# Norms between the phases of the first block of a two-block transformer kernel: where their squares, scales and sums are placed

## What is computed

```python
def rms_norm(x, w):
    y = x * rsqrt(mean(x * x, -1) + 1e-6)
    return y * w

for i in range(2):
    a_in = rms_norm(hs, norm_w[i, 0])
    mix = gated_deltanet(a_in, ...) if i == 0 else mlstm(a_in, ...)
    hs = hs + keep * rms_norm(mix, norm_w[i, 1])
    f = conv_ffn(rms_norm(hs, norm_w[i, 2]), w_up, conv_w, conv_b, w_down)
    hs = hs + keep * rms_norm(f, norm_w[i, 3])

def conv_ffn(h, w_up, conv_w, conv_b, w_down):      # 3 taps along the tokens
    u = causal_depthwise_conv(h @ w_up, conv_w) + conv_b
    return (silu(u[..., :2816]) * u[..., 2816:]) @ w_down
```

## Time and profile before

| | us |
|---|---|
| median of 3 runs | 1733.51 (1730.83 to 1734.56) |
| the profiled execution | 1733.33 |
| its span, first to last instruction | 1731.4 |
| TensorE busy | 1550.3 (90%) |
| VectorE busy | 970.8 (56%) |
| ScalarE busy | 788.9 (46%) |
| GpSimd busy | 338.4 (20%) |
| mean granted TensorE clock | 0.931 of full |

### The profile page before, as it was taken

The page is one execution under the profiler, slowest core; times in us unless marked ns, Lnnn a source line. Parts: engine busy times, 40 slices in busy tenths (PEclk is TensorE's granted clock), DMA queues, the critical chain, the costliest instruction groups (busy, mean ns, idle before and its releaser), DMA issues.

```text
span 1731.4 us, 32148 instructions
## 1 busy us (share of the span) xinstructions
PE 1550.3 (90%) x11757; PEld 1465.3 (85%) x11757; DVE 970.8 (56%) x1486; ACT 788.9 (46%) x1308; POOL 338.4 (20%) x351
## 2 busy tenths in 40 slices
PE   6999979979999899877999978689999985889997
PEld 5997967869999879576999978589999773789997
DVE  5874846546775454345777454554544546454443
ACT  5565423445554455335555344354443542454433
POOL 1203001104552000002665010013320002023300
PEclk9998958999999999778999989799999995899999
DMA  5551300233556425022555535036666430346662
GB/s 202 177 171 60 110 26 1 88 108 124 179 179 179 141 97 173 23 73 58 176 178 175 179 110 170 26 119 184 182 186 187 137 114 1 98 122 182 182 188 67
DMA packets 60992, 222.04 MB, mean 128 GB/s; under 512 B 6768, under 2 KB 7792, under 8 KB 60528
## 3 DMA queue, kind: packets, MB, share of 16 engines
q1 hardware_dynamic: 60768, 219.75, 41.6%
q10 hardware_dynamic: 144, 1.18, 0.2%
HBM read 219.85 MB, written 1.05 MB: 128 GB/s over the span
## 4 chain that ended last, share of the span: by engine, by line
PE 84%; DVE 9%; ACT 3%; issue 2%; DMA 1%; POOL 0%; SPq 0%; ACTq 0%; DVEq 0%
PE bank L404 23%; PE bank L406 23%; PE bank L405 23%; PE bank L467 3%; DVE y L537 1%; DVE y L495 1%; PE bank L1661 1%; PE bank L1772 1%; DVE wlo L370 1%; PE bank L1875 1%; PE bank L1856 1%; DVE y L1815 1%; PE bank L1062 1%; DMA par<-params 1%; PE bank L1042 1%
## 5 line engine op out<-in xcount | busy, mean ns | idle before, releaser
L370 DVE TENSOR_TENSOR wlo<-raw,whi 128x1024 fp32r<-128x1024 f32 x411 | 514.1, 1261 | 466.1 <-ACT whi L365 465.8
L404 PE MATMUL bank<-xs,whi 128*128 128x272 f32 (+1 forms) x2264 | 654.4, 289 | 29.8 <-POOL xs L396 19.4
L405 PE MATMUL bank<-xs,whi 128*128 128x272 f32 (+1 forms) x2264 | 651.7, 288 | 0.0
L406 PE MATMUL bank<-xs,wlo 128*128 128x272 f32 (+1 forms) x2264 | 650.2, 287 | 0.0
L365 ACT ACTIVATE whi<-raw 128x1024 fp32r<-128x1024 f32 x411 | 429.1, 1055 | 286.2 <-PE bank L406 282.8
L404 PEld LDWEIGHTS bank<-xs,whi 128*128 128x128 f32 x2264 | 431.6, 191 | 34.5 <-issue 22.9
L406 PEld LDWEIGHTS bank<-xs,wlo 128*128 128x128 f32 x2264 | 433.4, 191 | 0.0
L405 PEld LDWEIGHTS bank<-xs,whi 128*128 128x128 f32 x2264 | 433.0, 191 | 0.0
L404 PE MATMUL bank<-hf,whi 128*128 (+2 forms) x1024 | 295.0, 288 | 11.5 <-issue 10.5
L405 PE MATMUL bank<-hf,whi 128*128 (+2 forms) x1024 | 294.4, 288 | 0.0
L406 PE MATMUL bank<-hf,wlo 128*128 (+2 forms) x1024 | 294.1, 287 | 0.0
(11 more groups left out here) (410 smaller groups left out, 1288.0 us busy)
## 6 DMA issues: line engine op xcount, KB each, us to landing
raw<-stream SPq DMA_DIRECT2D x411, 512.0 KB, 3.6
con<-consts SPq DMA_DIRECT2D x1, 1284.5 KB, 7.8
big<-mla ACTq DMA_DIRECT2D x1, 1152.0 KB, 4.9
hs_sb<-hs SPq DMA_DIRECT2D x1, 1088.0 KB, 5.1
y_out<-hs_sb SPq DMA_DIRECT2D x8, 128.0 KB, 2.0
par<-params SPq DMA_DIRECT2D x1, 740.0 KB, 9.1
```

The source lines that it names most:

```text
L370: nc.vector.tensor_tensor(wlo[:, s, :], raw[:, s, :], whi[:, s, :].bitcast(F32), ALU.subtract).then_inc(block_split, 1)
L404: nc.tensor.matmul(out_, whi[:, slot, w], hi, start=start, stop=False)
L405: nc.tensor.matmul(out_, whi[:, slot, w], lo, start=False, stop=False)
L406: return nc.tensor.matmul(out_, wlo[:, slot, w], hi, start=False, stop=stop)
```

## The change

Seven parts; all but the second concern the first block only.

1. **Squares in the last row.** In a wide phase's last row each bank m is marked when its three matmuls are done; ScalarE squares it straight from the bank, and TensorE puts the sum matmul of bank m - 3 behind bank m's matmuls; four sums are left behind the row. VectorE scales the bank by the norm's weight while moving it to `y`, after its square. The last low half of a wide phase moves behind these eight.
2. **Three tiles k by k.** In every tiles phase the first three tiles run side by side: for chunk k high x high and low x high of all three (six matmuls), as soon as the high half of the chunk is there, and one step later the three matmuls with its low half. The other tiles follow as before, from tile 3.
3. **The residual.** VectorE alone adds: product with the factor, then the sum, chunk by chunk; ScalarE takes from it the high half, scaled by the next norm's weight, and the square.
4. **The pre norm's factor comes later.** The tiles get hs x weight without the factor; its sums run inside the three tiles' steps, and the factor is put on the finished banks: in up0 and up1 VectorE multiplies each bank in place before the convolution's first tap, in ml_in VectorE evicts every tile with the product.
5. **ml_in's gates** take hs and weights that GpSimd scales beforehand, behind the three tiles; five of the first tiles' low halves and evictions are put between the steps of the scans; the sigmoid runs in place behind VectorE's eviction.
6. **GpSimd** has no part of these norms any more (it keeps pre0 and the layer norms).
7. One explicit table load per boundary goes.

The diff, cut to its core:

```diff
-    def pe_tiles(pe, phase, g0, name, count=None):
+    def pe_tiles(pe, phase, g0, name, count=None, meanwhile=lambda k: None):
...
+        for k in range(KC + 1):
+            if k < KC:
+                w = slice(k * P, (k + 1) * P)
+                pe.wait_ge(*S("norm", "act").at(f"{name}_hi{k}"))
+                for j in range(AHEAD):
+                    o, s = rhs_out(g0 + j, phase), (b0 + j) % SLOTS
+                    if k == 0:
+                        pe.wait_ge(block_split, b0 + j + 1)
+                        pe.wait_ge(bank_free, g0 + j + 1)
+                    mm(o, whi[:, s, w], xs[:, k, 0:T], start=(k == 0), stop=False)
+                    mm(o, wlo[:, s, w], xs[:, k, 0:T], start=False, stop=False)
+            if k:
+                meanwhile(k - 1)
+                w = slice((k - 1) * P, k * P)
+                pe.wait_ge(*lo_done(name, k - 1))
+                for j in range(AHEAD):
+                    last = mm(rhs_out(g0 + j, phase), whi[:, (b0 + j) % SLOTS, w], xs[:, KC + k - 1, 0:T], start=False, stop=(k == KC))
+                    if k == KC:
+                        last.then_inc(block_used, 1)
...
+                if i is None and k == n - 1 and m < 7:
+                    last.then_inc(*S("wide", "pe").mark(f"{phase}_m{m}"))
+                    meanwhile(m)
...
+    SUM_LAG = 3
...
+    def post_in_row(pe, name, g):
+        def meanwhile(m):
+            if m >= SUM_LAG:
+                square_sum_pe(pe, name, g, m - SUM_LAG)
...
+    def post_act(act, name, g, phase):
         for m in range(KC):
-            act.wait_ge(bank_free, 8 + g - 8 + m + 1)
-            nc.scalar.activation(sq[:, m, :], y[:, m, :], ACT.Square)...
+            wide_done(act, phase, m)
+            nc.scalar.activation(sq[:, m, :], bank[(g - 8 + m) % 8][:, 0:T1], ACT.Square)...
...
+    def post_dve(dve, name, g, row, split):
         for m in range(KC):
-            nc.vector.tensor_copy(y[:, m, :], bank[(g - 8 + m) % 8][:, 0:T1]).then_inc(bank_free, 1)
+            dve.wait_ge(*S("norm", "act").at(f"{name}_{m}"))
+            nc.vector.tensor_scalar(y[:, m, :], bank[(g - 8 + m) % 8][:, 0:T1], pv("norm_w", row * KC + m), None, ALU.mult).then_inc(bank_free, 1)
+        split()
...
+    def add_y(dve, name, m):
+        v = S("norm", "dve")
+        nc.vector.tensor_tensor(y[:, m, :], y[:, m, :], rs[:, 1, :], ALU.mult).then_inc(*v.mark(f"{name}_y{m}"))
+        dve.wait_ge(*v.at(f"{name}_y{m}"))
+        nc.vector.tensor_tensor(hs[:, m, :], hs[:, m, :], y[:, m, :], ALU.add).then_inc(*v.mark(f"{name}_h{m}"))
+
+    def next_dve(dve, post, name, row):
+        def lo(m):
+            dve.wait_ge(*S("norm", "act").at(f"{name}_hi{m}"))
+            nc.vector.scalar_tensor_tensor(xs[:, KC + m, :], hs[:, m, :], pv("norm_w", row * KC + m), xs[:, m, :].bitcast(F32),
+                                           ALU.mult, ALU.subtract)...
         for m in range(KC):
+            add_y(dve, post, m)
+            if m:
+                lo(m - 1)
+        lo(KC - 1)
+
+    def next_act(act, post, name, row, g):
+        for m in range(KC):
+            act.wait_ge(*S("norm", "dve").at(f"{post}_h{m}"))
+            nc.scalar.activation(xs[:, m, :], hs[:, m, :], ACT.Copy, scale=pv("norm_w", row * KC + m))...
+            nc.scalar.activation(sq[:, m, :], hs[:, m, :], ACT.Square)...
+        act_scale(act, name, g, rs[:, 0, :], T1, D, eps_1)
...
     def ffn_act(act, f, g0):
...
             split_hi(act, b0 + t + AHEAD, ii)
             split_hi(act, b0 + t + AHEAD + 1, ii)
-            act.wait_ge(block_used, ii * 8 + (b0 + t + 2))
             act.wait_ge(conv_taken, ii * 8 + (c0 + t + 2))
             if f < 2:
+                act.wait_ge(*S("ffn", "dve").at(f"u{f}_{base}_{j}1", i))
                 conv_first(st, f"f{f}_{base}_{j}", tiles, 3, True)
...
     def ffn_dve(dve, f, g0):
...
-            split_lo(dve, b0 + t + AHEAD, ii)
-            split_lo(dve, b0 + t + AHEAD + 1, ii)
+            for a in range(2):
+                split_lo(dve, b0 + t + a + AHEAD, ii)
+                if f < 2:
+                    dve.wait_ge(block_used, ii * 8 + (b0 + t + a + 1))
+                    u = tiles[a][0][:, 0:T1]
+                    nc.vector.tensor_tensor(u, u, rs[:, 0, :], ALU.mult).then_inc(*st.mark(f"u{f}_{base}_{j}{a}"))
...
+    def ml_tile_dve(dve, t, split=True, i=0):
+        if split:
+            split_lo(dve, b0 + t + AHEAD, i)
+        dve.wait_ge(block_used, i * 8 + (b0 + t + 1))
+        nc.vector.tensor_tensor(dst, bank[(g0 + t) % 8][:, 0:T1], rs[:, 0, :], ALU.mult).then_inc(bank_free, 1)
...
+        between = {1: 3, 4: 4, 7: 5}
+        b = scan(dve, s, "b", f_row, t4_row, ALU.add, T1, lambda n: ml_tile_dve(dve, between[n]) if n in between else None)
...
-        pre_pe(pe, "pre1", G["pre1"])
-        pe_tiles(pe, "up0", G["up0"], "pre1")
-        pe_wide(pe, "down0", G["down0"], ffn_ready(0))
+        pe_tiles_rest(pe, *pe_tiles(pe, "up0", G["up0"], "pre1", None, pre_in_wave("pre1")))
+        pe_wide(pe, "down0", G["down0"], ffn_ready(0), meanwhile=post_in_row(pe, "post1", G["post1"]))
```

More of the change, by code:

```diff
@@ L519, in mix_dve, with square_sum_pe @@
                                     ).then_inc(*S("norm", "dve").mark(f"{name}_lo{k}"))
+    SUM_LAG = 3
+    def square_sum_pe(pe, name, g, m):
+        if m == 0:
+            pe.wait_ge(bank_free, g + 1)
+        pe.wait_ge(*S("norm", "act").at(f"{name}_{m}"))
+        last = nc.tensor.matmul(bank[g % 8][:, 0:T1], ones, sq[:, m, :], start=(m == 0), stop=(m == KC - 1))
+        if m == KC - 1:
+            last.then_inc(*S("norm", "pe").mark(name))
+    def post_in_row(pe, name, g):
+        def meanwhile(m):
+            if m >= SUM_LAG:
+                square_sum_pe(pe, name, g, m - SUM_LAG)
+        return meanwhile
@@ L1571, in ml_gates_act, with scan @@
         A(s_row, s_row, ACT.Ln, bias=1.0).then_inc(*s.mark("lf"))
-    def scan(dve, s, tag, src, other, op, T):
+    def scan(dve, s, tag, src, other, op, T, meanwhile=lambda n: None):
         step, n = 1, 0
@@ L1588, in ml_gates_dve @@
         ts, stt, tt = nc.vector.tensor_scalar, nc.vector.scalar_tensor_tensor, nc.vector.tensor_tensor
+        for t in range(2):
+            split_lo(dve, FIRST_BLOCK["ml_in"] + t + AHEAD)
+        dve.wait_ge(*S("norm", "act").at("pre2_scale"))
+        for n, row in enumerate((i_row, f_row)):
+            dve.wait_ge(*S("gates", "pe").at(f"ml{n}"))
+            tt(row, bank[(G["ml_g"] + n) % 8][0:MH, 0:T1], rs[0:MH, 0, :], ALU.mult).then_inc(bank_free, 1)
+        ml_tile_dve(dve, 0, False)
+        ml_tile_dve(dve, 1, False)
+        ml_tile_dve(dve, 2)
         dve.wait_ge(*a_.at("lf"))
@@ L1594, in ml_gates_dve @@
         dve.wait_ge(*s.at("logf"))
-        b = scan(dve, s, "b", f_row, t4_row, ALU.add, T1)
-        split_all(dve, split_lo, "ml_in", 4, 4)
+        between = {1: 3, 4: 4, 7: 5}
+        b = scan(dve, s, "b", f_row, t4_row, ALU.add, T1, lambda n: ml_tile_dve(dve, between[n]) if n in between else None)
         stt(c_row, i_row, GATE_CAP, b, ALU.mult, ALU.subtract).then_inc(*s.mark("c"))
@@ L1606, in ml_in_act, with ml_gate_weights_pool @@
     def ml_in_act(act):
-        g0, b0 = G["ml_in"], FIRST_BLOCK["ml_in"]
-        for turn in range(2):
-            with act.Fori(0, (2, 1)[turn]) as i:
-                for j in range(8):
-                    split_hi(act, b0 + 16 * turn + j + AHEAD, i)
-                    act.wait_ge(block_used, i * 8 + (b0 + 16 * turn + j + 1))
-                    nc.scalar.activation(big[:, i * 8 + (16 * turn + j), :], bank[(g0 + j) % 8][:, 0:T1],
-                                         (ACT.Copy, ACT.Sigmoid)[turn]).then_inc(bank_free, 1)
+        g0, b0, a_ = G["ml_in"], FIRST_BLOCK["ml_in"], S("ml", "act")
+        for t in range(AHEAD):
+            split_hi(act, b0 + t + AHEAD)
+        ml_gates_act(act)
+        split_all(act, split_hi, "ml_in", AHEAD, 16 - AHEAD)
+        for t in range(16, 24):
+            split_hi(act, b0 + t + AHEAD)
+            act.wait_ge(bank_free, 8 + g0 + t + 1)
+            nc.scalar.activation(big[:, t, :], big[:, t, :], ACT.Sigmoid).then_inc(*a_.mark("og" if t == 23 else f"og{t}"))
+    def ml_gate_weights_pool(pool):
+        w = pv("ml_gates", 0, KC * 8).rearrange("p (k n) -> p k n", k=KC)
+        nc.gpsimd.tensor_tensor(w, w, alone(pv("norm_w", 4 * KC, KC), 8), ALU.mult).then_inc(*S("gates", "pool").mark("mlw"))
     def ml_pe(pe):
@@ L2350, in _ @@
         nc.scalar.preload_act_table_set(LN_EXP)
[L2351 to L2353 removed]
+        post_act(act, "post0", G["post0"], "gdn_out")
+        next_act(act, "post0", "pre1", 2, G["pre1"])
         nc.scalar.preload_act_table_set(SILU)
```

170 lines of the change are left out of this document (86 added, 84 removed).

## The result

The changed kernel takes 1783.51 us (median of 4 runs, 1782.99 to 1788.34), against 1732.3 for the kernel before in the same comparison (4 runs, 1730.83 to 1734.56): a ratio of 1.030, 95% interval 1.0284 to 1.0316. It is slower by 51 us, where 34 were forecast. The profiled execution took 1783.89 us, with a span of 1782.1.

What follows compares the result with a forecast made beforehand. TensorE's work plus its stands or lower clock set the time, with a ScalarE-VectorE ring nearly filling two tiles. Terms 49.2 + 1.5 - 4 - 5.5 - 7 = +34 us on 1733.3 gave 1767 us; range 1744 to 1785.

Steps and rivals of the forecast that it cites:

- The ring: up0 and up1: ScalarE and VectorE handing work round per tile pair takes 7.40 us against TensorE's 6.01; 24.6 us later each.
- The last row of down0 stands on the taps: First row of down0 in the prediction: TensorE stands 6 us in its seventh group, waiting for VectorE's taps.
- Squares inside the row gain nothing: Boundary before up0: squares and sums in gdn_out's last row end at 374.9 against 374.2 before, costing 0.7 us.
- The bubble behind the wave: up0: after the first three tiles run side by side (the wave), TensorE stands 4.4 us before the fourth tile.
- I count none of them as a loss: Clock: forecast gaps of 2.5 us before a wave, 4.4 behind it and 1.3 per pair were priced at nothing.
- The small idles: Pairs of the new ring: by the skill's rule small idles could swing the clock, putting every pair at risk; not counted.
- the clock falls in the pairs or waves: Slower rival, chance 0.06: eight waves or bubbles losing 3 us each add 24, 1791 us; whole projections up to 193, 1960.
- ev_in: Phase behind boundary b2: the wave ends at 1025.4, the fourth tile starts at 1027.0 against 1032.59 before; minus 5.5 us.
- up2 and up3: Later up-projections: tiles start on the first high half, no longer on GpSimd's low half; minus 3.6 us twice, 7.
- gdn_in: First three tiles all end at 33.1, so the following ring starts later, tile 3 ending at 36.1; plus 1.5 us.
- ml_in: Tile 3 starts 7.5 us earlier, five low halves delayed by scans give back some 3.5; minus 4 us.
- a ring of 7.07: Lighter sum for up0 and up1: low halves at 1.24 and products at 0.37, given as 1751 us.

Runs made afterwards that it cites:

- run 1: Changed kernel, up0 and up1 pairs reordered: both products before the first low half, second low half behind the taps, second high half behind first taps; 1711.29 us.
- run 3: Changed kernel without VectorE's product in up0 and up1, first taps waiting for TensorE only, the factor left out of the result; 1710.97 us.
- run 6: Changed kernel with only VectorE's order edited in up0 and up1: both products before both low halves, ScalarE as it was; 1719.45 us, ratio 0.992.
- run 4: Kernel before the change with only the first three tiles of every tiles phase run side by side, chunk by chunk; 1716.82 us, ratio 0.991.
- run 2: Changed kernel with the up0 and up1 product moved to SBUF scratch, first taps waiting for TensorE only, the factor left out; 1755.92 us.
- run 9: Run 1's kernel, tile 3's block split inside the wave, later up0/up1 splits one block earlier, ml_in's product before the low half from tile 8; 1707.98 us.
- run 10: Changed kernel with one edit in ml_in: from tile 8 on, VectorE's product comes before the next block's low half; 1777.4 us.

## Why the prediction was right, and where it was short

Direction, mechanism and range held: 1783.5 lies inside 1744 to 1785, 1.5 us under its upper edge, and one of the four runs (1788.34) lies above it. The forecast was 16.5 us short. Point by point, on the profiled executions (+50.7 us of span, forecast +34):

- **The ring.** Forecast 7.40 us a turn. Measured: the first pair's last tap ends at 399.62, the last pair's at 554.76, so 7.39 on average over 21 turns (forecast 399.4 and 554.8). That the ring binds, and where it closes, is right; that the number fits to 0.01 is in part luck. In the ordinary turn of 7.30 the low halves hold VectorE for 1.15 and 1.13 us where 1.35 was put for each, 0.42 too much, and the taps begin 1.00 behind the end of the second product where 0.62 was put, 0.38 too little; every fourth turn takes 7.82, which no term held. The absolute times fit so well by luck too: the changed kernel reached this boundary 1.5 us ahead of the kernel before (365.8 for 367.3) and lost as much to the clock in the wave. Runs 1, 3 and 6 show that without this ring nothing is lost in these stages.
- **The last row of down0 stands on the taps.** Forecast 6 us, measured 6.21.
- **Squares inside the row gain nothing.** Forecast +0.7 against the old order. Sums ended at 373.5, 8.8 us behind the last split of gdn_out (364.74); forecast 8.7. In run 4, with the old order, they end 8.0 behind it (373.87 for 365.89).
- **The bubble behind the wave.** Forecast 4.4 us, measured 4.37. The third tile ended 26.0 us behind the start of the last row (390.7 for 364.7), forecast 24: most of that is the clock of the next point.
- **The step that failed: "I count none of them as a loss."** I had read that 4 us of standing cost the clock, saw gaps of 4.4 and 6 us coming, and priced them at nothing (the 6 us in down0's first row stand in the forecast, but not in its list of gaps). The wave ran its first 3.1 us at 0.55, which costs 3.1 x 0.45 = 1.4 us (the wave took 14.5 us instead of 13.0), and down0 its first 7.2 us at 0.58, which costs 3.0. Together that is 4.4 us, and each up and down stage is 4.1 longer than forecast. The tile behind the bubble ran at 0.50 too, but the ring hid that.
- **The small idles.** The rule of the Trainium skill (TensorE: Matmul & The Clock Gate, "A second HAM failure mode: psum-queue depth-cycling") put every pair at risk; in 148 us with stands of about 1.1 us in nearly every pair the granted clock was 1.00, so this trace does not show it. The rival "the clock falls in the pairs or waves" had 3 us each for eight waves or bubbles, 24 in all; measured in the two up and down stages were two waves at 1.4 and two first rows at 3.0, 8.8 us, and nothing in the pairs behind the first. (ml_in's wave lost another 1.2, 3.0 us at 0.59.)
- **Terms of the other stages.** ev_in -6.4 (forecast -5.5), up2 and up3 -6.1 (-7). gdn_in lost 0.9 us up to the table load behind it (forecast 1.5), but the mixer stage that follows took 240.2 us for 242.6, which no term held. ml_in -1.6 for -4 (its last tile, counted from down0's last row, ended 2.4 us earlier). With the same code in ml_in the stage took 97.3 to 100.5 us in seven profiles, and this scatter goes with the clock: a mean granted clock of 1.00 in the two of 97.3 (runs 2 and 3), 0.98 in the two of 98.9, 0.97 in the three of 100.4 and 100.5, the changed kernel among them. At 1.00 the term is -4.7 against the 102.0 before (at 0.97), so here too it was the clock that the forecast had left out.
- **What no term held.** mLSTM +7.4 and even mixer +3.6: granted clock 0.67 for 0.78 and 0.71 for 0.80, at equal work. That is 11 us of the 16.5. Two executions of one kernel differ by 3 in the mLSTM stage, so some of it can be chance; what lowers the clock there no run shows, and this largest part of the miss stays open.

As a sum of differences from the forecast: up and down stages +8.2, mLSTM +7.4, even mixer +3.6, ml_in +2.4, up2 and up3 +0.9, gdn_in and its mixer -3.0, ev_in -0.9, the rest -2.1: 16.5. Beside this, two sums of the prediction do not hold together: a ring of 7.07 (low halves at 1.24, products at 0.37) gives 1754, not 1751, and the range is said to hold the bounds of the low half, while the upper of these, 3.14 per pair, gives 1786 by its own sum, past 1785.

## What to carry to other kernels

Where two engines hand work to each other once per pair of tiles, write the ring out with every handover before adding a step to it, and compare it with the bound engine's time: 0.9 us of products cost 1.4 us a pair here in one order and nothing in another. Put the instruction that waits for the bound engine ahead of the work that feeds that engine's next tiles, not between its halves. And when a forecast contains a stand of the size that a row shows to cost the clock, price what follows it at the lower level: 1.4 to 3.0 us each here, and put the shorter stands down as a chance rather than a certainty.

## What the runs showed of the hardware

- TensorE's granted clock behind stands, in the changed kernel: 2.7 us of standing at 1.00 were followed by 3.1 us at 0.55, 4.4 us by 5.0 at 0.50, 6.2 us by 7.2 at 0.58; stands of 1.1 us once per 7.3 us, eighteen times over, left it at 1.00. One and the same stand of 2.6 us, in front of ev_in, was followed by 5.0 us at 1.00 in one profile and at 0.66 in another of the same kernel.
- A stretch of thin work can draw different clocks with the same instructions: behind the same stand, the first 12 us of the mLSTM stage ran at 0.57 in run 9 and at 1.00 in run 10, and the stage took 82.5 to 95.7 us over twelve profiles.
- VectorE's product with both operand and result in the same bank takes 0.442 us (median of 88, 0.434 to 0.445), close to the 0.436 of a product of bank and SBUF; with both operands in SBUF it took 0.43, 0.65 or 1.00 in run 2, and the low half of 128x1024 behind it 1.21 without GpSimd beside it and 1.82 to 1.84 with GpSimd's subtraction (0.78) beside its start.
